# Stick-breaking attention computed for two heads at a time on the tensor array, with paired filter taps and a reordered Hyena stage

## The chip, the cores and the metric

The kernel runs on one core of one Trainium2 chip. The metric is the device time of one execution in microseconds (us), smaller is better; the figure used is the median of several executions.

## The reference, cut to what matters

Two transformer blocks run one after the other on 512 tokens of width 1024, in fp32. The parts that the change touches:

```python
# block 1: 8 heads of 64; attention over strictly earlier tokens
z = q @ k.T * 64 ** -0.5                       # per head, 512 x 512, lower triangle by blocks of 128
log_not = where(s < t, log_sigmoid(-z), 0)
suffix  = reverse_cumsum(log_not) - log_not
a = where(s < t, exp(log_sigmoid(z) + suffix), 0)
o = a @ v
# block 2: differential attention (4 heads, two score maps of 64 each, 512 x 768) beside a Hyena mixer
s = q @ k.T * 64 ** -0.5; a = softmax(s); w = a[0] - lam * a[1]
h = sin(freq * (z @ w1 + b1)); h = sin(freq * (h @ w2 + b2)); h = sin(freq * (h @ w3 + b3)); h = h @ w4
z = gate * (long_conv(z, fft(h)) + skip * z)   # twice, on 3 * 512 projected channels with a short convolution
```

Projections, branch gates, two feed-forward layers and the norms around them fill the rest of the time and are not touched.

## The kernel before

All matrix products are kept near fp32 accuracy: an operand is split into a high and a low half (`..h`, `..l`, wh, wl), and `mm3` issues high times high, high times low and low times high. Weights stream in units of 1,024 columns through four raw buffers and four slots: SyncE issues the load, ScalarE makes wh (L1081), VectorE makes wl (L1651), and for the units listed in `POOL_LOW` GpSimd makes wl instead (L2274). Units of the DFT matrices (kind `pre`) come ready-made by DMA from GpSimd's queue. Every engine has its own program, a fixed list in order; semaphores join them. Nothing is reordered at run time: an engine that waits holds back all that is written behind the wait.

**Filter taps.** `first(k)` and `second(k)` for k = 0 to 19 interleave the input projections with small side work. `filter_layer` makes three sine layers of 64 channels. `taps(i, o)` then issues, for d = 0 and 1, one plain fp32 matmul that contracts over 64 channels, both from partitions 0 to 63. A plain fp32 matmul shows as two records in the trace. VectorE multiplies each result by a decay, GpSimd forms sum and difference (L2311). Steps k = 16 to 19 are `mix`.

**Stick-breaking attention.** A step n is one head h and one block s of 128 keys; its width w is 512 minus 128 s queries, so w = 128, 256, 384, 512 in the order s = 3, 2, 1, 0. The list SB runs head by head, 32 steps. For each step:

- TensorE `scores(n)`: three fp32r matmuls over 64 partitions (0 to 63 for even heads, 64 to 127 for odd ones), into one of four PSUM banks (ZB).
- ScalarE: Abs, Exp, Ln (L1173, L1175, L1177). VectorE: softplus (L1764). GpSimd: the triangular mask (L2344). VectorE: high and low half (L1768, L1770).
- TensorE `later_keys(n)`: products with the constant matrices NEG add the suffix sums to the same bank.
- ScalarE: Exp (L1184). GpSimd: mask. TensorE `values(n)`: one plain fp32 matmul with 64 output partitions.

The order is `scores(n)`, `later_keys(n - 2)`, one `early` part (two k-tiles of a gate projection, six matmuls; 24 parts in all), `values(n - 4)`. The bank of step n is free again when its second Exp (`sb_e2`) is done.

**Differential attention.** `diff_scores(n)` already issues the two maps of a head in turns, map 0 from partitions 0 to 63 and map 1 from 64 to 127. VectorE takes two row maxima (L2062), each followed by a small multiply by -0.125 (L2064), ScalarE the exponentials (L1444), VectorE the weighted difference of the maps (L2076, both operands in SBUF). Two parts of the Hyena projections lie between steps. Units are converted in odd steps, the short convolution (L2083) runs in even ones.

**Hyena stage.** Twelve column groups of the projection (24 matmuls each) are needed. Eight are computed inside the differential attention, groups 8 and 9 at the start of the Hyena stage, group 10 before the last two inverse steps of order 0, group 11 after them. Each order runs `forward` for four frequency blocks, VectorE's products with the spectrum (`spectral`, L2158 to L2162), and `backward`. Between the orders, a chain over ScalarE, VectorE and GpSimd (`acc`, gate, `fold(1)`) makes the input of order 1.

Of the kernel before, what the change touches and what calls it, by code (L numbers as in the profile page):

```python
# [18 lines left out]
BEFORE = 10  # L19
# [8 lines left out]
def plan():  # L28
# [69 lines left out]
    for o in range(2):  # L98
# [48 lines left out]
for _u in range(NU):  # L147
# [9 lines left out]
    AT["dft_f", 0, 0][0][0] + SLOTS - 1 <= u < AT["w_out_2", 0, 0][0][0] + SLOTS - 1  # L157
# [8 lines left out]
class Waits:  # L166
# [5 lines left out]
    def wait_ge(self, name, n):  # L172
        s, before = self.find(name)
        if n > 0 and self.past.get(s.name, 0) < before + n:
# [30 lines left out]
          "high": (("qk_hi", 8), ("mx_hi", 4), ("ot_hi", 8), ("ef_hi", 4), ("g_hi", 12), ("ff_hi", 32), ("qk2_hi", 8),  # L205
                   ("ys_hi", 16), ("ug_hi", 22)),
          "low": (("qk_lo", 8), ("mx_lo", 4), ("ot_lo", 8), ("g_lo", 12), ("qk2_lo", 8)),
          "v_side": (("f_red", 21), ("tap_mul", 16), ("pg_pool", 4), ("gm_nv", 4), ("mx_z", 2)),
          "v_gate": (("eg_raw", 6), ("eg_mul", 4), ("ef_v", 8), ("g_mul", 18)),
          "v_score": (("sb_sp", 32), ("df_mx", 64)),  # L210
# [61 lines left out]
def program(nc, a):  # L272
    ctx = ExitStack()
    with ctx:
# [54 lines left out]
        W4 = at("w4", 168, [64, CHUNK])  # L329
        NEG = at("neg", 174, [P, 2, P], F32R)  # L330
# [39 lines left out]
        EG = [BC[0][:, 0:S], BC[0][:, S:], BC[1][:, S:], BC[1][:, 0:S], T(6), T(7)]  # L370
# [5 lines left out]
        SB = [(h, s) for h in range(8) for s in (3, 2, 1, 0)]  # L376
# [15 lines left out]


# [31 lines left out]
        def tensor_program(engine):  # L425
# [131 lines left out]
            def filter_layer(l):  # L557
# [7 lines left out]
                mm(PS[0:64, b, :], TMP[0:n, 1, 64 * l:64 * l + 64], src, True, True).then_inc(sem("p_filt"), 1)  # L565
# [39 lines left out]
            def scores(n):  # L605
                h, s = SB[n]
                w, t0 = S - P * s, P * s
                pr = slice(64 * (h % 2), 64 * (h % 2) + 64)
                b = bank(("z", n), "sb_e2", n + 1, ZB)
                e.wait_ge("qk_lo", 8)  # L610
                kk = (QKh[pr, 4 + h // 2, t0:t0 + P], QKl[pr, 4 + h // 2, t0:t0 + P])
                mm3(PS[:, b, :w], kk, (QKh[pr, h // 2, t0:], QKl[pr, h // 2, t0:]), True, True).then_inc(sem("p_sc"), 1)
# [14 lines left out]
            def values(n):  # L627
                h, s = SB[n]
                w, t0 = S - P * s, P * s
                pr = slice(64 * (h % 2), 64 * (h % 2) + 64)  # L630
                if s == 3:
                    bank(("o", h), "ot_lo", h + 1, OB)
                e.wait_ge("v_ev", 4)
                e.wait_ge("sb_k2", n + 1)
                mm(PS[pr, BANK["o", h], t0:], V1[:, s, h * 64:h * 64 + 64], T(3 + n % 3, w), s == 3,
                   s == 0).then_inc(sem("p_val"), 1)
# [14 lines left out]
            for k in range(20):  # L651
                if k >= 18:
                    scores(k - 18)
                first(k)
                second(k)


            for n in range(len(SB) + 4):
                if 2 <= n < len(SB):
                    scores(n)  # L660
                if 0 <= n - 2 < len(SB):
                    later_keys(n - 2)
                if n % 3 < 2:
                    early(n - (n + 1) // 3)
                if 0 <= n - 4 < len(SB):
                    values(n - 4)
# [9 lines left out]
            for m in range(EARLY):  # L676
                b = bank(("ef", m), "ef_v", 4 * m + 1)
                for k in range(4):
                    e.wait_ge("ot_lo", 2 * k + 2)
# [283 lines left out]
            for j in range(4):  # L963
                hyena_turn(j)
# [1782 lines left out]
```

## Time and profile before

| | |
|---|---|
| median of 3 executions | 1582.85 us (1582.1 to 1583.59) |
| profiled execution | 1580.21 us, its span 1578.5 us |
| TensorE busy | 1507.5 us, 96% |
| VectorE busy | 877.3 us, 56% |
| ScalarE busy | 622.5 us, 39% |
| GpSimd busy | 291.1 us, 18% |
| granted TensorE clock, mean | 0.991 |
| attention of block 1, 145.6 to 250.5 us | 104.9 us |
| differential attention, 945 to 1052 us | 107 us |
| Hyena stage, 1057.2 to 1153.4 us | 96.2 us |

Busy times are sums over instructions. The span is the profiled stretch on the core; the execution's own time adds 1.7 us around it. TensorE matmuls are pipelined: a record of 0.39 us is followed by the next after about 0.23 us, so what a matmul costs is the distance from its start to the next start, and not its duration.

### The profile page before, as it was taken

What the parts mean: (1) busy time and instruction counts of PE and PEld (TensorE: products, weight loads), DVE (VectorE), ACT (ScalarE), POOL (GpSimd) and SP (SyncE); (2) the same over time, 40 slices, a digit from 0 to 9 for tenths busy, and PEclk for the clock granted to TensorE, in tenths of its full rate; (3) what the DMA queues carried; (4) which work ended last, traced back from release to release, by engine and by line L of the source; (5) the groups of instructions that cost most, each with busy time, mean ns of one, the idle gap of its engine ahead of it and who ended that gap; (6) DMA issues with size and microseconds to landing.
All of it is one profiled execution on the core that took longest, in us unless ns stands there. A gap on an engine that the chain in (4) does not pass through costs nothing.

```text
span 1578.5 us, 17718 instructions
## 1 busy us (share of the span) xinstructions
PE 1507.5 (96%) x6878; PEld 1200.0 (76%) x6878; DVE 877.3 (56%) x1429; ACT 622.5 (39%) x978; POOL 291.1 (18%) x289
## 2 busy tenths in 40 slices
PE   6999999999989999999997998989798999999998
PEld 5767667888868878888886876668576888888886
DVE  5445556555467654565447438856766455334534
ACT  5535664222353322334335325644344333223332
POOL 0253111110122200122004310006441110111101
PEclk9999999999999999999999999999999999999999
DMA  7342002654345544545326221124442322323221
GB/s 232 126 146 81 27 28 93 235 166 148 132 134 173 174 147 140 178 145 178 113 100 208 91 67 40 41 94 139 131 154 69 108 93 95 99 89 106 94 94 54
DMA packets 53262, 187.87 MB, mean 119 GB/s; under 512 B 6104, under 2 KB 6616, under 8 KB 52986
## 3 DMA queue, kind: packets, MB, share of 16 engines
q1 hardware_dynamic: 47386, 165.76, 32.3%
q0 software_dynamic: 4736, 16.78, 3.2%
q10 hardware_dynamic: 1056, 4.19, 0.7%
q8 instruction: 55, 0.90, 0.2%
q14 instruction: 29, 0.24, 0.0%
HBM read 174.12 MB, written 12.58 MB: 118 GB/s over the span
## 4 chain that ended last, share of the span: by engine, by line
PE 80%; DVE 9%; issue 4%; ACT 4%; POOL 3%; DMA 0%; SPq 0%; DVEq 0%; POOLq 0%; ACTq 0%
PE PS L447 79%; POOL TMP L2311 2%; DVE smallring L2062 1%; DVE TMP L2083 1%; PE PS L458 1%; ACT em L1444 1%; DVE wl L1651 1%; DVE TMP L2158 1%; DVE em L2076 1%; POOL y L2321 0%; DMA X<-in_x 0%; ACT wh L1081 0%; DVE accm L1631 0%; ACT wt L1435 0%; POOL wl L2274 0%
## 5 line engine op out<-in xcount | busy, mean ns | idle before, releaser
L1651 DVE TENSOR_TENSOR wl<-raw,wh 128x1024 fp32r<-128x1024 f32 x219 | 283.8, 1299 | 283.1 <-ACT wh L1081 283.0
L447 PE MATMUL PS<-HTh,wh 128*128 128x512 f32 x1056 | 419.7, 397 | 12.4 <-DVE TMP L1977 5.8
L447 PE MATMUL PS<-HTh,wl 128*128 128x512 f32 x1056 | 413.0, 391 | 0.0
L447 PE MATMUL PS<-HTl,wh 128*128 128x512 f32 x1056 | 412.8, 391 | 0.0
L1081 ACT ACTIVATE wh<-raw 128x1024 fp32r<-128x1024 f32 x228 | 239.1, 1053 | 286.2 <-PE PS L447 251.9
L447 PEld LDWEIGHTS PS<-HTh,wh 128*128 128x128 f32 x1056 | 199.5, 189 | 61.3 <-issue 11.0
L447 PEld LDWEIGHTS PS<-HTh,wl 128*128 128x128 f32 x1056 | 199.0, 188 | 42.8
L447 PEld LDWEIGHTS PS<-HTl,wh 128*128 128x128 f32 x1056 | 199.5, 189 | 38.5 <-issue 0.5
L447 PE MATMUL PS<-wh,FFh 128*128 128x512 f32 x432 | 169.1, 392 | 0.0
L447 PE MATMUL PS<-wh,FFl 128*128 128x512 f32 x432 | 168.2, 389 | 0.0
L447 PE MATMUL PS<-wl,FFh 128*128 128x512 f32 x432 | 168.1, 389 | 0.0
L1631 DVE SCALAR_TENSOR_TENSOR accm<-raw,small,accm 128x256 f32<-128x256 f32 x224 | 108.0, 516 | 3.4
L2234 DVE SCALAR_TENSOR_TENSOR TMP<-PS,pp,TMP 128x255 f32<-128x255 f32 (+1 forms) x132 | 52.1, 395 | 80.3 <-ACT TMP L1583 76.4
L447 PEld LDWEIGHTS PS<-wh,FFl 128*128 128x128 f32 x432 | 81.1, 188 | 17.1
L447 PEld LDWEIGHTS PS<-wl,FFh 128*128 128x128 f32 x432 | 81.1, 188 | 16.5
L447 PEld LDWEIGHTS PS<-wh,FFh 128*128 128x128 f32 x432 | 81.1, 188 | 16.5
L2384 POOL TENSOR_TENSOR FFl<-TMP,FFh 128x512 fp32r<-128x512 f32 x32 | 41.6, 1299 | 240.1 <-ACT FFh L1295 240.1
L2466 POOL TENSOR_TENSOR FFl<-TMP,FFh 128x512 fp32r<-128x512 f32 x22 | 28.5, 1294 | 211.8 <-ACT FFh L1590 211.8
L1295 ACT ACTIVATE FFh<-TMP 128x512 fp32r<-128x512 f32 x32 | 20.2, 632 | 66.5 <-DVE TMP L1917 66.5
L1291 ACT ACTIVATE TMP<-PS 128x512 f32<-128x512 f32 x32 | 19.0, 595 | 57.7 <-PE PS L447 57.7
L2083 DVE SCALAR_TENSOR_TENSOR TMP<-PS,pp,TMP 128x255 f32<-128x255 f32 (+1 forms) x72 | 28.4, 395 | 16.0 <-ACT TMP L1452 13.9
L2474 POOL TENSOR_TENSOR X<-X,TMP 128x512 f32<-128x512 f32 x14 | 19.7, 1434 | 90.1 <-DVE TMP L2249 90.1
(320 smaller groups left out, 2163.7 us busy)
## 6 DMA issues: line engine op xcount, KB each, us to landing
raw<-in_ws SPq DMA_DIRECT2D x268, 512.0 KB, 3.8
taps<-TMP SPq DMA_DIRECT2D x16, 256.0 KB, 2.5
tab<-in_spec POOLq DMA_DIRECT2D x8, 512.0 KB, 5.6
raw<-taps SPq DMA_DIRECT2D x8, 512.0 KB, 3.7
kd<-TMP POOLq DMA_DIRECT2D x16, 256.0 KB, 4.3
wh<-in_wd POOLq DMA_DIRECT2D x8, 512.0 KB, 3.9
wl<-in_wd POOLq DMA_DIRECT2D x8, 512.0 KB, 4.6
kf<-kd SPq DMA_DIRECT2D x8, 512.0 KB, 3.9
```

The lines of the kernel that those rows point to most:

```text
L447: return nc.tensor.matmul(out, l, r, start=start, stop=stop, skip_group_check=True)
L1081: act(WH[u % SLOTS][:, :n], RAW[i % RAWS][:, :n], ACT.Copy).then_inc(sem("w_hi"), 1)
L1291: act(T(q % 2), PS[:, BANK["ff", hf, m], :], ACT.Relu).then_inc(sem("ff_relu"), 1)
L1295: act(FFh[:, m, :], T(2 + q % 2), ACT.Copy).then_inc(sem("ff_hi"), 1)
L1631: stt(acc, r[:, k % 4, :], c, acc, ALU.mult, ALU.add).then_inc(sem("mod_acc"), 1)
L1651: tt(WL[k][:, :n], RAW[RAW_AT["unit", u, 0] % RAWS][:, :n], f32(WH[k][:, :n]), ALU.subtract).then_inc(sem("lo_dve"), 1)
L2083: stt(out[:, do], ps[:, di], pp("hy_conv_w_2", 12 * w + j), out[:, do], ALU.mult, ALU.add).then_inc(sem("hc_v"), 1)
L2234: stt(z[:, do], ps[:, di], pp("ffn_conv_w_2", 22 * w + m), z[:, do], ALU.mult, ALU.add).then_inc(sem("uc_v"), 1)
L2311: tt(T(k), T(3), T(5), op).then_inc(sem("tap_ed"), 1)
L2384: tt(FFl[:, q % 16, :], T(2 + q % 2), f32(FFh[:, q % 16, :]), ALU.subtract).then_inc(sem("ff_lo"), 1)
L2466: tt(FFl[:, m - first_m, :], T(m % 4), f32(FFh[:, m - first_m, :]), ALU.subtract).then_inc(sem("ug_lo"), 1)
L2474: tt(x, x, T(4 + q % 4), ALU.add).then_inc(sem("dn_xp"), 1)
```

## The change

- **Two heads at once.** SB now runs over pairs of heads. `scores(p)` issues the three products of the two heads in turns (upper rows, lower rows), `values(p)` two matmuls into output partitions 0 to 63 and 64 to 127 of one bank. The output copy OTh and OTl is made once per pair, on 128 partitions.
- **Order.** `scores(p + 2)` now stands behind `later_keys` and the early parts of pair p, `values(p - 1)` last. There are still four score banks, so `scores(p + 2)` needs both second Exps of pair p.
- **NEG** moves to another address, and its copy from ScalarE's step 14 to step 19, behind the last `mix`.
- **Paired taps.** The filter layers are computed on 128 output partitions (weights and biases repeated), w4 lies as 128 x 1024, and the two matmuls of a tap step contract over the upper and the lower 64 rows.
- **Differential attention.** The scale 0.125 goes into the rotated queries, the maximum is negated by the reduction itself, the small multiply L2064 is gone.
- **Weights' low halves.** POOL_LOW now begins with unit 3 of the Hyena projections instead of unit 3 of the DFT: GpSimd makes wl for groups 3 to 7, and for the later groups.
- **Hyena order.** Group 8 stands before the last two inverse steps of order 0, groups 9 and 10 behind them, group 11 before the last two inverse steps of order 1; their convolutions and transposes move accordingly.

```diff
-BEFORE = 10
+BEFORE = 8
...
-        if o == 0:
-            pack(colmajor("w_in_2", 1536 + 10 * P, 1))
+        pack(colmajor("w_in_2", 1536 + (8 if o == 0 else 11) * P, 1))
         pack(inv[2] + inv[3], "pre")
         if o == 0:
-            pack(colmajor("w_in_2", 1536 + 11 * P, 1))
+            pack(colmajor("w_in_2", 1536 + 9 * P, 2))
...
 POOL_LOW = [u for u in range(NU) if u not in PRE and (
-    AT["dft_f", 0, 0][0][0] + SLOTS - 1 <= u < AT["w_out_2", 0, 0][0][0] + SLOTS - 1
+    AT["w_in_2", 0, 1536][0][0] + SLOTS - 1 <= u < AT["w_out_2", 0, 0][0][0] + SLOTS - 1
...
-        SB = [(h, s) for h in range(8) for s in (3, 2, 1, 0)]
+        SB = [(2 * p + i, s) for p in range(4) for s in (3, 2, 1, 0) for i in range(2)]
...
             def taps(i, o):
+                n = 4 * i + 2 * o
                 for d in range(2):
-                    n = 4 * i + 2 * o + d
-                    b = bank(("tap", n), "tap_mul", n + 1, RING2)
-                    c = o * 1024 + d * 512
-                    e.wait_ge("f_sin", 3)
-                    e.wait_ge("d_w4", 48)
-                    mm(PS[:, b, :], TMP[0:64, 4, i * P:(i + 1) * P], W4[:, c:c + 512], True, True).then_inc(sem("p_tap"), 1)
+                    bank(("tap", n + d), "tap_mul", n + d + 1, RING2)
+                e.wait_ge("f_sin", 3)
+                e.wait_ge("d_w4", 48)
+                for d in range(2):
+                    pr = slice(64 * d, 64 * d + 64)
+                    mm(PS[:, BANK["tap", n + d], :], TMP[pr, 4, i * P:(i + 1) * P], W4[pr, o * S:(o + 1) * S], True,
+                       True).then_inc(sem("p_tap"), 1)
...
+                for i in range(2):
+                    bank(("z", 2 * p + i), "sb_e2", 2 * p + i + 1, ZB)
                 e.wait_ge("qk_lo", 8)
+                for j, (k, q) in enumerate(((QKh, QKh), (QKh, QKl), (QKl, QKh))):
+                    for i in range(2):
+                        pr = slice(64 * i, 64 * i + 64)
+                        m = mm(PS[:, BANK["z", 2 * p + i], :w], k[pr, 4 + c, t0:t0 + P], q[pr, c, t0:], j == 0, j == 2)
...
+                for i in range(2):
+                    c = (h + i) * 64
+                    mm(PS[64 * i:64 * i + 64, BANK["o", h // 2], t0:], V1[:, s, c:c + 64], T(3 + (2 * p + i) % 4, w), s == 3,
+                       s == 0).then_inc(sem("p_val"), 1)
...
+            for p in range(PAIRS + 1):
+                if p < PAIRS:
+                    later_keys(2 * p)
+                    later_keys(2 * p + 1)
+                    for f in EARLY_AT(p):
+                        early(f)
+                if p + 2 < PAIRS:
+                    scores(p + 2)
+                if p:
+                    values(p - 1)
...
-                    nc.vector.reduce_max(r[:, m:m + 1], s, axis=mybir.AxisListType.X).then_inc(sem("df_mx"), 1)
-                    e.wait_ge("df_mx", 4 * n + 2 * m + 1)
-                    ts(r[:, m:m + 1], r[:, m:m + 1], -0.125, None, ALU.mult).then_inc(sem("df_mx"), 1)
+                    nc.vector.reduce_max(r[:, m:m + 1], s, axis=mybir.AxisListType.X, negate=True).then_inc(sem("df_mx"), 1)
...
-                if o == 0:
-                    hyena_group(10)
+                hyena_group(8 + 3 * o)
                 backward(o, 2)
                 backward(o, 3)
+                hyena_turn(8 + 3 * o)
                 if o == 0:
-                    hyena_group(11)
+                    hyena_group(9)
+                    hyena_group(10)
                     sub_scale(2)
```

## Rows read from the trace of the kernel before

**Rows 1.** The page, busy time, share of the span and instructions of each engine.

```profile
PE 1507.5 (96%) x6878; PEld 1200.0 (76%) x6878; DVE 877.3 (56%) x1429; ACT 622.5 (39%) x978; POOL 291.1 (18%) x289
```

**Rows 2.** Windows over four stages: length, busy time of each engine, clock, DMA.

```profile
145.60:250.50 104.90, 103.75 (x462) 66.08 (x458) 58.62 (x114) 65.36 (x140) 19.11 (x64) 1.00 0.10 31
945.00:1052.00 107.00, 94.60 (x517) 69.27 (x517) 84.39 (x176) 59.49 (x103) 1.13 (x2) 1.00 0.18 55
1057.20:1106.90 49.70, 49.70 (x246) 41.22 (x245) 29.49 (x52) 23.08 (x44) 26.18 (x24) 0.97 0.45 147
1106.90:1153.40 46.50, 33.96 (x133) 24.52 (x132) 34.85 (x51) 16.01 (x27) 26.38 (x20) 0.93 0.36 115
```

**Rows 3.** Timeline of TensorE in block 1's attention: start, duration, instruction.

```profile
162.19 0.86 PE L447 MATMUL PS<-TMP,V 128*64 128x384 f32 x2
162.98 0.49 PE L447 MATMUL PS<-QKh 64*128 64x512 f32 x1
...
163.87 0.33 PE L447 MATMUL PS<-sph,neg 128*128 128x128 f32 x1
...
165.92 1.07 PE L447 MATMUL PS<-TMP,V 128*64 128x512 f32 x2
166.92 0.32 PE L447 MATMUL PS<-QKh 64*128 64x128 f32 x1
...
167.40 0.33 PE L447 MATMUL PS<-sph,neg 128*128 128x128 f32 x1
```

**Rows 4.** Timeline of TensorE at small matmuls: taps, two mix steps, differential scores.

```profile
65.16 1.98 PE L447 MATMUL PS<-w,TMP 64*128 64x512 f32 x4
...
131.77 1.07 PE L447 MATMUL PS<-pt,wpool 64*64 64x512 f32 x4
...
140.16 1.09 PE L447 MATMUL PS<-wst,bc 128*64 128x128 f32 x16
...
970.43 0.50 PE L447 MATMUL PS<-KTh,QTh 64*128 64x512 f32 x2
```

**Rows 5.** Groups of ScalarE instructions, 145.6 to 250.5 us.

```profile
L1177 ACT ACTIVATE TMP<-TMP 128x384 f32<-128x384 f32 (+3 forms) x30 | 14.3, 478 | 1.0
L1184 ACT ACTIVATE TMP<-PS 128x128 f32<-128x128 f32 (+3 forms) x32 | 13.7, 427 | 3.3 <-PE PS L447 3.1
L1173 ACT ACTIVATE TMP<-PS 128x384 f32<-128x384 f32 (+3 forms) x30 | 13.2, 442 | 24.0 <-PE PS L447 23.9
```

**Rows 6.** Timeline of TensorE at the start of that attention.

```profile
154.30 0.33 PE L447 MATMUL PS<-sph,neg 128*128 128x128 f32 x1 [1.15 <-DVE spl L1770]
```

**Rows 7.** Timeline of GpSimd, the gate of the second mix.

```profile
147.86 1.28 POOL L2353 TENSOR_TENSOR TMP<-TMP,gu 128x512 f32<-128x512 f32 x1 [1.47 <-DVE TMP L1732]
```

**Rows 8.** Groups of VectorE instructions, 945 to 1052 us.

```profile
L2064 DVE TENSOR_SCALAR smallring<-smallring 128x1 f32<-128x1 f32 x32 | 4.9, 154 | 1.1
```

**Rows 9.** Timeline of ScalarE, VectorE, GpSimd: one unit's conversion, two subtracts, a GpSimd subtract.

```profile
970.17 1.06 ACT L1081 ACTIVATE wh<-raw 128x1024 fp32r<-128x1024 f32 x1
...
972.00 1.02 DVE L2076 SCALAR_TENSOR_TENSOR em<-em,smallring,em 128x768 f32<-128x768 f32 x1
...
1083.41 0.68 DVE L2162 TENSOR_TENSOR TMP<-TMP 128x512 f32<-128x512 f32 x1
...
1095.70 2.83 POOL L2274 TENSOR_TENSOR wl<-raw,wh 128x1024 fp32r<-128x1024 f32 x1
...
1096.20 2.88 DVE L2162 TENSOR_TENSOR TMP<-TMP 128x512 f32<-128x512 f32 x1
```

**Rows 10.** Timeline of ScalarE at the start of the Hyena stage.

```profile
1067.64 2.04 ACT L1475 ACTIVATE U<-PS 128x512 f32<-128x512 f32 x4
1069.70 1.28 ACT L1502 ACT_TABLE_LOAD   x1
```

**Rows 11.** Timeline of TensorE between the orders of the Hyena stage.

```profile
1126.95 2.07 PE L447 MATMUL PS<-ndg,cst 128*128 128x512 f32 x2 [5.01 <-DVE TMP L2083]
...
1150.58 0.50 PE L447 MATMUL PS<-ysh,wh 128*128 128x512 f32 x1 [3.05 <-POOL ysl L2432]
```

More of the change, by code:

```diff
@@ L390, in program, with EARLY_AT @@
                 (0, slice(256, 511), slice(257, 512)), (2, slice(257, 512), slice(256, 511)))
+        PAIRS = len(SB) // 2
+        def EARLY_AT(p):
+            return range((3 * p + 1) // 2, (3 * p + 4) // 2)
         def HSLOT(j):
@@ L651, in tensor_program @@
             for k in range(20):
-                if k >= 18:
-                    scores(k - 18)
+                if k == 18:
+                    scores(0)
                 first(k)
                 second(k)
[L658 to L666, printed above, removed]
+            scores(1)
+            for p in range(PAIRS + 1):
[8 more added lines that the diff above has]
+                    values(p - 1)
             for q in range(4):
@@ L961, in sub_scale @@
                 mm(PS[:, b, :], ONES, NDG[:, :], True, True).then_inc(sem("p_sn"), 1)
-            for j in range(4):
-                hyena_turn(j)
-            hyena_group(8)
-            for j in range(4, 8):
+            for j in range(8):
                 hyena_turn(j)
             sub_sums()
-            hyena_group(9)
-            hyena_turn(8)
             def forward(o, f):
@@ L1198, in scalar_program @@
             for k in range(20):
-                if k >= 18:
-                    scores(k - 18)
+                if k == 18:
+                    for i in range(2):
+                        scores(i)
                 first(k)
                 second(k)
-            for n in range(len(SB) + 4):
-                if 2 <= n < len(SB):
-                    scores(n)
-                if 0 <= n - 2 < len(SB):
-                    later_keys(n - 2)
-                if n % 3 < 2:
-                    early(n - (n + 1) // 3)
-                if 0 <= n - 4 < len(SB):
-                    values(n - 4)
+            for i in range(2, 4):
+                scores(i)
+            for p in range(PAIRS + 1):
+                if p < PAIRS:
+                    later_keys(2 * p)
+                    later_keys(2 * p + 1)
+                    for f in EARLY_AT(p):
+                        early(f)
+                if p + 2 < PAIRS:
+                    scores(2 * p + 4)
+                    scores(2 * p + 5)
+                if p:
+                    values(p - 1)
             weights(unit("w_br_pool", 0, P) + SLOTS - 1)
@@ L1791, in vector_program @@
                 first(k)
-                if k >= 18:
-                    scores(k - 18)
+                if k == 18:
+                    for i in range(2):
+                        scores(i)
                 second(k)
-            for n in range(len(SB) + 4):
-                if 2 <= n < len(SB):
-                    scores(n)
-                if n % 3 < 2:
-                    early(n - (n + 1) // 3)
-                if 0 <= n - 4 < len(SB):
-                    values(n - 4)
+            for i in range(2, 4):
+                scores(i)
+            for p in range(PAIRS + 1):
+                if p < PAIRS:
+                    for f in EARLY_AT(p):
+                        early(f)
+                if p + 2 < PAIRS:
+                    scores(2 * p + 4)
+                    scores(2 * p + 5)
+                if p:
+                    values(p - 1)
             weights(unit("w_br_pool", 0, P) + SLOTS - 1)
@@ L2717 @@
         elif n.startswith("hy_b") or n == "hy_freq_2":
-            ppv[0:64, o] = i[n].reshape(-1)
+            ppv[:, o] = np.tile(i[n].reshape(-1), 2)
         else:
@@ L2731 @@
         "lam": np.concatenate([i[n].reshape(-1) for n in ("lam_q1_2", "lam_q2_2", "lam_k1_2", "lam_k2_2")]),
[L2732 to L2734 removed]
+        "hy_w4_2": i["hy_w4_2"][0].reshape(64, 2, 2, S).transpose(2, 0, 1, 3).reshape(P, D),
+    }
+    for n in ("hy_w1_2", "hy_w2_2", "hy_w3_2"):
+        arrays[n] = np.tile(i[n][0], (1, 2))
     arrays = {k: np.ascontiguousarray(v) for k, v in arrays.items()}
```

181 lines of the change are left out of this document (83 added, 98 removed).

## The prediction

> **What bounds the kernel now.** I read the page first: TensorE is busy for 1507.5 of 1578.5 us [rows 1], so work taken off TensorE comes out of the span wherever TensorE doesn't wait. Then a table of windows shows where it waits. In the attention of block 1 (145.6 to 250.5 us) TensorE is busy 103.75 of 104.9 us while ScalarE works 65.36 and VectorE 58.62 [rows 2]: TensorE is the limit, with about a third of ScalarE's time in reserve. In the differential attention it is busy 94.60 of 107 us, and VectorE 84.39 [rows 2]: there a VectorE and ScalarE chain sets the pace at several steps. In the second half of the Hyena stage it is busy 33.96 of 46.50 us, so 12.5 us are waits; in the first half it never waits (49.70 of 49.70) [rows 2]. The rest of the kernel isn't edited. The timeline gives the price of single matmuls, as start to next start.
>
> **Taps.** Today a tap step is four records of 1.98 us, of which the last 0.07 overlaps what follows: 1.91 us [rows 4]. Is a pair in two halves of the array concurrent? The mix step at 131.77 us does that now: four records of the same width, two matmuls in opposite 64 x 64 quarters, in 1.07 us against 1.98 [rows 4]. I take 0.86 us saved for each of eight steps, 6.8 us (bounds: 0 if the form with all 128 columns didn't overlap, 7.3 at 0.91 each). Both banks are now awaited at once; the old second matmul had waited for the same multiply, and steps lie some 7 us apart, so nothing is late. GpSimd's running sums start when the last tap is out, so they move forward with TensorE. The sine layers with 128 outputs stream as many columns as before, and their DMAs are small: nothing.
>
> **Attention of block 1, TensorE's part.** The value matmul of width 384 costs 162.98 - 162.19 = 0.79 us, of width 512 166.92 - 165.92 = 1.00 [rows 3]; by this step of 0.21 the other widths are 0.58 and 0.37, 2.74 us per head. The score step of width 512 costs 163.87 - 162.98 = 0.89, of width 128 167.40 - 166.92 = 0.48 [rows 3]; the widths between, by a straight line, 0.75 and 0.62, also 2.74 per head. Eight heads: 21.9 us of each. Does pairing halve them? For scores the trace holds the new form itself: the differential scores issue two fp32r matmuls from upper and lower rows, and the pair of width 512 takes 0.50 us [rows 4], as long as the single one (0.49 [rows 3]), and the next pair starts 0.3 us later. So 10.95 us. For values the nearest row is the mix at 140.16: sixteen records of width 128 alternate between left and right columns in 1.09 us [rows 4], where the two records of a lone value matmul of that width need 0.37, so 0.064 us a record against about 0.18. So 10.95 us again, together 21.9. Bounds: 10.95 if only scores overlap; 23.3 if the switch into and out of the small form, about 0.09 us, is also saved on half the steps beyond what the slots contain.
>
> Here the Trainium skill, "TensorE: Matmul & The Clock Gate", section "Measured speedup vs the span model", gives less: three column tiles reached 2.38 times, 0.79 per tile. By that rate a pair is 1.59 times as fast, and values would save 8.1 us where the rows give 10.95; no row of width 512 in this form settles it.
>
> **The same stage, the other engines.** Two things are new. First, ScalarE and TensorE are now coupled once per pair: `scores(p + 2)` needs the second Exps of pair p, which stand on ScalarE behind the three functions of pair p + 1. ScalarE needs 0.442 + 0.478 + 0.478 + 0.427 = 1.83 us per step (Exp and Ln alike) [rows 5], 3.65 per pair; with TensorE's score pair (0.69) and two handoffs, some 0.3, the loop is 4.6 us. TensorE's own pair costs (104.9 - 21.9) / 16 = 5.2 us. On average TensorE stays the limit, but the widest pair takes about 1.35 times ScalarE's mean, 4.9 + 0.9 + 0.3 = 6.1 us, and meets an iteration of TensorE with little work (one early part, short `later_keys`): about 4 to 4.7. The iterations beside it have slack, so I charge 0.65 us per head pair, 2.6 us. Second, NEG. `later_keys(0)` now waits for a copy behind the last mix: VectorE's addition (about 0.6), GpSimd's product 1.28 [rows 7], two ScalarE copies (about 1.0) and handoffs (0.4), 3.3 us after the mix, less 0.6 for the score pair in between, 2.7 us idle where 1.15 is idle now [rows 6]: 1.6 lost. The stage's gain: 21.9 - 2.6 - 1.6 = 17.7 us (bounds 7 and 22).
>
> **Differential attention.** 32 multiplies of 0.154 us vanish, 4.9 us in all [rows 8]; start to start each costs about 0.13, 0.27 per step, and it counts in the 11 or so steps that VectorE paces: 3.0 us. The move of wl is a loss. VectorE's wl (odd steps) lies in time in which VectorE waits for the second exponential anyway, so taking it away gives nothing. On GpSimd it takes 2.4 to 2.83 us, and while it runs a VectorE operation with both operands in SBUF stands still: L2162 took 2.88 us beside GpSimd's 2.83, alone 0.68 [rows 9]. The conversion wh ends at 971.23, GpSimd would run to about 973.7, and VectorE's L2076, both operands in SBUF, is due at 972.00 for 1.02 us [rows 9]; it would end at about 974.6 instead of 973.0. That is 1.6 us in a chain that paces TensorE. Five units move (groups 3 to 7); by where their wh ends, three meet L2076: 4.7 us. Net loss 1.7, of which the steps with a value product absorb part: I take 1.0 lost (bounds: 3 gained if nothing collides, 5 lost if all five do).
>
> The Trainium skill, "SBUF — State Buffer", section "SBUF: two separate sides", states the same as a rule and so speaks against this part: VectorE with two SBUF inputs and GpSimd share an exclusive pair of ports, and the loser blocks for a whole instruction. The trace agrees (2.88 beside 0.68).
>
> **Hyena stage.** Groups 8 and 9 leave the first half, 24 matmuls of 0.227 us each, 10.9 us, where TensorE never waits. Two covers go with them. `forward(0, 0)` needs banks that ScalarE frees after its fold copies: about 0.6 us idle. `sub_scale(0)` follows a chain with four copies of 2.04 us and a table load of 1.28 [rows 10], which group 9 hid: about 2.3 us idle. In the second half groups 9 and 10 fill the time of the fold where group 11 alone stood, and VectorE has one convolution ahead of `spectral(4)` instead of two: the waits of 5.01 and 3.05 [rows 11] go, about 5.5 us of group 9 or 10 and 5.4 of group 11 take their place. The 12.5 us of waits are enough for the 10.9 us, but little is left over, and turn 8 and turn 11 now precede the copies that start the fold: even. Gain 10.9 - 0.6 - 2.3 = 8.0 us (bounds 3 and 11).
>
> **Sum.** 6.8 + 17.7 - 1.0 + 8.0 = 31.5 us. The profiled execution took 1580.2 us, so 1548.7; the median shown lies 2.6 higher, at 1582.85: forecast 1551.3 us. Measured differences under 0.2% (3 us) say nothing here.
>
> **Rivals.**
> - **The coupling to ScalarE paces the attention** (loop per pair near 5.9 us instead of 5.2). The handoffs that I put at 0.3 speak for or against it: ScalarE at 58.4 of then 85 us is no bound by itself. Stage gain 8 instead of 17.7: 1561. Chance 0.15.
> - **Values or taps don't overlap in their new form** (128 rows by 64 columns, width 512): 10.95 or 6.8 less, 1558 to 1562. The mix rows speak against it. Chance 0.07. The page's rate of 1.59 alone would give 1554, inside my forecast.
> - **GpSimd meets nothing in the differential attention, and the Hyena gaps close better**: 4 and 3 us more, 1544. Chance 0.17.
> - **The Hyena order gives back what it takes** (a fold starved by the turns before it, the first half's waits longer): 5 less or nothing at all, 1557 to 1559. Chance 0.05.
> - **Slower: only one pair in flight.** If the four banks let no score pair start before the former pair's second Exps were through, a pair would take its whole latency: scores 0.7, ScalarE's three functions 2.8, VectorE and GpSimd about 2, `later_keys` 1.6, Exp 0.9, handoffs 0.5, 8.5 us; sixteen make 136 us for 104.9, 31 lost against 13.8 gained elsewhere: 1600. It decides from 7.4 us per pair on ((104.9 + 13.8) / 16). Four banks hold two pairs, so it should not come. Chance 0.03.
>
> **How the numbers follow.** The forecast has 0.53; its own range is 1546 to 1556. The range of 0.8 takes in the ScalarE loop and the better Hyena case: 1542 to 1563. Faster by over 0.2%: all but the slow case and a remnant, 0.95; same 0.02; slower 0.03.
>
> **What the profile after would show.** Tap steps of about 1.07 us for four records; score pairs that start about 0.9 us (width 512) before what follows; value records x4 in 1.07 us; the stage of block 1 about 87 us, with short waits on ScalarE's L1184 group at the widest pairs and one of 2.7 us before the first `later_keys`; L2064 gone; L2076 of 2.6 us at some steps beside GpSimd's L2274; TensorE waiting 2 to 3 us early in the Hyena stage and no more 5 us between the orders. I am wrong if value pairs stay at twice 1.00 us, if ScalarE holds every pair, or if the differential attention changes by more than 5 us.

## The result, and the profile after

The changed kernel takes 1557.43 us (median of 4, 1555.99 to 1559.42) against 1582.59 in the same comparison: ratio 0.9841 [0.9826, 0.9855], 25.2 us faster. The forecast was 1551.3 us, with a range of 1542 to 1563. The profiled execution took 1557.35 us, its span 1555.6.

The page of the changed kernel, busy time, share and instructions, beside [rows 1]:

```profile
PE 1482.2 (95%) x6878; PEld 1191.4 (77%) x6878; DVE 864.5 (56%) x1386; ACT 619.0 (40%) x974; POOL 308.7 (20%) x296
```

The windows over the same stages, beside [rows 2]; block 1's attention, the differential attention, and the two parts of the Hyena stage. Columns: length, busy time of TensorE, its weight loads, VectorE, ScalarE, GpSimd, granted clock, DMA share, GB/s.

```profile
137.50:227.10 89.60, 81.49 (x465) 58.73 (x461) 54.04 (x108) 62.70 (x138) 20.24 (x64) 0.98 0.11 36
...
920.50:1040.70 120.20, 106.27 (x528) 74.41 (x529) 78.13 (x137) 57.23 (x101) 14.92 (x9) 0.94 0.15 49
1040.70:1081.80 41.10, 38.05 (x186) 30.80 (x185) 30.30 (x46) 22.54 (x42) 26.46 (x21) 0.96 0.40 129
1081.80:1130.30 48.50, 43.97 (x185) 34.46 (x184) 33.88 (x57) 18.33 (x30) 30.12 (x24) 0.96 0.46 152
```

From the last mix matmul to the end of its attention, block 1 went from 104.9 to 89.6 us, and TensorE now waits there for 8 us. The differential attention, cut at the same matmuls in both, went from 112.2 to 120.2 us: it got **slower by 8 us**, at a granted clock of 0.94 (1 is 2.4 GHz, 0.5 is 1.2 GHz) where it had 1.00. From there to the last normalisation, 107.1 us became 102.6.

The new forms on TensorE in the timeline, beside [rows 3, 4]: values of width 384 and 512, a score pair of width 384, a tap step.

```profile
97.24 1.13 PE L453 MATMUL PS<-w,TMP 64*128 64x512 f32 x4
98.30 0.50 PE L453 MATMUL PS<-HTh,wh 128*128 128x512 f32 x1
...
163.90 0.87 PE L453 MATMUL PS<-TMP,V 128*64 128x384 f32 x4
164.70 0.33 PE L453 MATMUL PS<-sph,neg 128*128 128x128 f32 x1
...
168.08 0.44 PE L453 MATMUL PS<-QKh 64*128 64x384 f32 x2
168.35 0.33 PE L453 MATMUL PS<-QKl,QKh 64*128 64x384 f32 x2
168.52 0.34 PE L453 MATMUL PS<-QKh,QKl 64*128 64x384 f32 x2
168.79 1.08 PE L453 MATMUL PS<-TMP,V 128*64 128x512 f32 x4
169.80 0.33 PE L453 MATMUL PS<-sph,neg 128*128 128x128 f32 x1
```

Start to next start, two heads' values now take 0.80 and 1.01 us where one head's took 0.79 and 1.00; a score pair of width 384 takes 0.71, as one head's did before (148.63 to 149.34 us there), where the prediction had put 0.75 between its rows; a tap step takes 1.06 in place of 1.91. So a pair costs what one costs, to within 0.02 us for values and scores, and a tap step is 0.10 us more than half of the old one. The rate of three column tiles (of 32 columns each) that the prediction cited from the Trainium skill ("TensorE: Matmul & The Clock Gate", "Measured speedup vs the span model"), 1.59 for a pair, does not carry over to two tiles of 64 columns: 2 x 1.00 / 1.01 = 1.98 here.

The start of the attention in TensorE's timeline; in brackets how long it sat idle before, and for whom. One wait was foreseen there, for NEG:

```profile
136.66 1.09 PE L453 MATMUL PS<-wst,bc 128*64 128x128 f32 x16
141.03 0.39 PE L453 MATMUL PS<-QKh 64*128 64x256 f32 x2 [3.27 <-ACT V L1145]
...
142.73 0.30 PE L453 MATMUL PS<-sph,neg 128*128 128x128 f32 x1 [1.08 <-ACT neg L1176]
...
144.37 0.63 PE L453 MATMUL PS<-HTh,wl 128*128 128x512 f32 x1
144.79 0.63 PE L453 MATMUL PS<-HTh,wh 128*128 128x512 f32 x1
...
146.46 0.39 PE L453 MATMUL PS<-HTl,wh 128*128 128x512 f32 x1
146.69 0.39 PE L453 MATMUL PS<-HTh,wl 128*128 128x512 f32 x1
```

`scores(1)` needs banks that hold block 1's V, and ScalarE evicts them only behind its copy of the mix, which waits for GpSimd:

```profile
138.31 0.63 ACT L1174 ACTIVATE OTh<-TMP 128x512 fp32r<-128x512 f32 x1 [5.55 <-POOL TMP L2372]
138.84 2.04 ACT L1145 ACTIVATE V<-PS 128x512 f32<-128x512 f32 x4
```

Behind the two waits six matmuls run at 0.43 us each, the 1.2 GHz level, where they cost 0.23 at 2.4 GHz: another 1.3 us. The whole stretch at that level lasts 3.4 us (142.9 to 146.3), so it costs 1.7.

The differential attention in the timelines of VectorE, GpSimd and TensorE, in this order:

```profile
948.27 0.27 DVE L2093 TENSOR_SCALAR smallring<-smallring,rd,small 128x1 f32<-128x1 f32 x1
948.58 2.93 DVE L2095 SCALAR_TENSOR_TENSOR em<-em,smallring,em 128x768 f32<-128x768 f32 x1
951.43 1.81 DVE L2083 TENSOR_REDUCE smallring<-PS 128x1 f32<-128x768 f32 x2
```
```profile
948.30 2.39 POOL L2289 TENSOR_TENSOR wl<-raw,wh 128x1024 fp32r<-128x1024 f32 x1 [9.51 <-ACT wh L1095]
```
```profile
954.43 0.49 PE L453 MATMUL PS<-KTh,QTh 64*128 64x512 f32 x2 [2.12 <-ACT em L1464]
```

This is the collision foretold from [rows 9]: L2095 (L2076 before), a product of two SBUF operands, takes 2.93 us beside GpSimd's subtraction and 1.02 alone. It happens three times, at 936.7, 948.6 and 979.0 us, the number that was foretold. Each time the reductions behind it, and so ScalarE's exponentials and TensorE's next scores, come late. The subtractions of the other two units that moved, at 926.21 and 968.99 us, meet L2095 too, but it has begun 0.5 us before them. Then it keeps its 1.02 us, and GpSimd's takes 2.79 and 2.77 in place of 2.39. So the one that starts second is held up. VectorE's row and GpSimd's:

```profile
968.50 1.02 DVE L2095 SCALAR_TENSOR_TENSOR em<-em,smallring,em 128x768 f32<-128x768 f32 x1
```
```profile
968.99 2.77 POOL L2289 TENSOR_TENSOR wl<-raw,wh 128x1024 fp32r<-128x1024 f32 x1 [18.29 <-ACT wh L1095]
```

### The profile page after: what moved, and what is told of

The parts are those of the page before. It is cut to its first block, busy times and chain, and to the rows that moved or that the text cites. A ratio compares the mean times of both kernels' runs of the same rounds, so it can differ in the third digit from the quotient of the medians.

```text
span 1555.6 us, 17697 instructions
## 1 busy us (share of the span) xinstructions
PE 1482.2 (95%) x6878; PEld 1191.4 (77%) x6878; DVE 864.5 (56%) x1386; ACT 619.0 (40%) x974; POOL 308.7 (20%) x296
## 4 chain that ended last, share of the span: by engine, by line
PE 84%; DVE 8%; ACT 5%; issue 2%; POOL 1%; DMA 0%; SPq 0%; ACTq 0%; DVEq 0%; POOLq 0%
PE PS L453 83%; ACT em L1464 1%; DVE TMP L2102 1%; DVE em L2095 1%; DVE TMP L2173 1%; PE PS L464 1%; DVE wl L1666 1%; DVE smallring L2083 1%; DVE TMP L1719 0%; ACT wh L1095 0%; DMA X<-in_x 0%; DVE accm L1646 0%; ACT TMP L1189 0%; POOL wl L2289 0%; ACT wt L1455 0%
## 5 line engine op out<-in xcount | busy, mean ns | idle before, releaser
L1666 DVE TENSOR_TENSOR wl<-raw,wh 128x1024 fp32r<-128x1024 f32 x212 | 274.4, 1299 | 281.8 <-ACT wh L1095 281.3
L2249 DVE SCALAR_TENSOR_TENSOR TMP<-PS,pp,TMP 128x255 f32<-128x255 f32 (+1 forms) x132 | 52.1, 394 | 78.4 <-ACT TMP L1598 74.5
L2289 POOL TENSOR_TENSOR wl<-raw,wh 128x1024 fp32r<-128x1024 f32 x16 | 39.5, 2468 | 123.7 <-ACT wh L1095 123.7
```

What stands on the lines that cost most here:

```text
L1666: tt(WL[k][:, :n], RAW[RAW_AT["unit", u, 0] % RAWS][:, :n], f32(WH[k][:, :n]), ALU.subtract).then_inc(sem("lo_dve"), 1)
L2249: stt(z[:, do], ps[:, di], pp("ffn_conv_w_2", 22 * w + m), z[:, do], ALU.mult, ALU.add).then_inc(sem("uc_v"), 1)
L2289: tt(WL[k][:, :n], RAW[RAW_AT["unit", u, 0] % RAWS][:, :n], f32(WH[k][:, :n]), ALU.subtract).then_inc(sem("lo_pool"), 1)
```

## The experiments

Medians are of 4 or 5 executions, of 12 for the negated maximum. The kernel before had medians of 1581.6 to 1582.6 us in the various comparisons. The 95% interval of a ratio is 2 to 3 us of kernel time to either side (1.3 for the negated maximum), so medians of two versions that are less than about 3 us apart don't tell them apart. The traces say more about single stages. But stretches in which TensorE runs at 1.2 GHz come and go from one trace to another, 1.7 us or 3.4 us each.

**Groups 3 to 7 back on VectorE**, the rest as changed:

```diff
-    AT["w_in_2", 0, 1536][0][0] + SLOTS - 1 <= u < ...
+    AT["dft_f", 0, 0][0][0] <= u < ...
```

> The changed kernel, with one part taken back: VectorE again makes the low halves of the weights of Hyena groups 3 to 7 (five units), GpSimd keeps the later ones. Theory (port and clock): in the changed kernel the weighted difference of the maps took 2.9 us instead of 1.02 at three steps beside GpSimd's subtract, and three stretches at half clock (1.2 GHz) stand in the same stage, where the kernel before had none. Both should go: 3 x 1.9 us and about 3 x 1.4 us, 8 to 10 us faster than the changed kernel, so 1547 to 1550 us; from the first differential scores to the first Hyena transpose about 110 us instead of 120.2. Rival 1 (VectorE's own load): with five conversions back on VectorE, which paces this stage, the gain is eaten, within 2 us of 1557.4. Rival 2 (only the port): 5.7 us faster, 1551.7, the half-clock stretches stay.

Measured: 1549.27 us (1548.29 to 1549.46), ratio 0.9791 [0.9776, 0.9805], 8.2 us faster than the changed kernel. Windows of the stage, and TensorE's waits in it, first this kernel's, then the changed kernel's:

```profile
923.10:1031.60 108.50, 99.87 (x529) 71.49 (x530) 77.67 (x142) 57.09 (x101) 2.20 (x4) 1.00 0.16 54
```
```profile
PE PS L453 <- ACT em L1464: 4.0, 8, 0.9
```
```profile
PE PS L453 <- ACT em L1464: 9.2, 7, 2.1
```

The time is inside the range of the theory. The stage is 11.7 us shorter than in the changed kernel. 5.2 us of that are waits for ScalarE's exponentials; the rest is the clock, since TensorE's busy time for the same matmuls falls from 106.27 to 99.87 us, 6.4 us, and 5.2 + 6.4 = 11.6. Not all of the 6.4 belongs to the collisions. The changed kernel's stage has four stretches at 1.2 GHz, of about 3.4 us and so 1.7 us lost each. Windows behind the first, second and third collision, then at the other two places:

```profile
942.50:946.00 3.50, 3.47 (x25) 3.07 (x26) 3.43 (x6) 1.86 (x3) 0.00 (x0) 1.00 0.00 0
955.40:958.70 3.30, 3.30 (x10) 1.52 (x8) 2.27 (x3) 0.00 (x0) 0.00 (x0) 0.50 0.02 5
986.10:989.40 3.30, 3.30 (x6) 1.51 (x5) 1.94 (x3) 0.00 (x0) 0.00 (x0) 0.50 0.02 5
...
921.20:924.70 3.50, 3.50 (x16) 2.74 (x13) 2.34 (x6) 1.88 (x5) 0.00 (x0) 0.51 0.00 0
...
1034.00:1037.00 3.00, 3.00 (x4) 1.22 (x5) 0.24 (x1) 0.00 (x0) 0.00 (x0) 0.50 0.00 0
```

TensorE waits 2.13, 2.12 and 2.13 us behind the three collisions, and only the second and third wait are followed by the low level. All five traces of kernels with this edit and the paired attention agree in this, and none of the seven traces without the edit has a low stretch at these places.

The stretch at 921 us lies ahead of every collision; five of the thirteen traces have it, two of them of kernels without the edit. The one at 1034 us stands in three of the five and its cause is open. So what the traces tie to the three collisions is 5.2 us of waits and 2 x 1.7 us of clock, 8.6 us, close to the 8.2 us by which the kernels differ. (Two of the runs below, scores head by head and both taps from the lower rows, have the stretch at the start and not the one at 1034 us: their stage takes 118.4 us, against 109.5 in the two kernels without collisions that have the same stretch, 8.9 us.) The clock is two fifths of what a collision costs here.

**That edit alone on the kernel before:**

> The kernel before with one edit of the change alone, the lower bound of POOL_LOW: the low halves of the weights of Hyena groups 3 to 9 go to GpSimd while the differential attention runs. In the changed kernel that edit cost 8.2 us (11.7 in the stage), by three weight products on VectorE that took 2.92 us in place of 1.02 and a low clock behind the waits that follow. Theory: the collision of GpSimd's 2.4 us subtraction with VectorE's product of two SBUF operands is the edit's own and needs nothing else of the change: the stage of the differential attention goes from 112.2 to 120 to 124 us, the kernel to 1588 to 1592 us. Rival: it only costs where VectorE and ScalarE have been sped up around it (the two scalings gone), so that the kernel before has slack for it: 1581 to 1585 us.

Measured: 1591.53 us (1591.44 to 1593.65), ratio 1.0062 [1.0049, 1.0076], 9.6 us slower. Window of the stage, and its waits beside 7.8 us in the kernel before:

```profile
947.40:1070.10 122.70, 104.44 (x528) 74.44 (x529) 83.49 (x169) 59.53 (x103) 19.06 (x9) 0.96 0.15 48
```
```profile
PE PS L447 <- ACT em L1444: 13.7, 9, 2.5
```

122.7 us against 112.2, by 5.9 us more of waits and 4.6 us more of busy time at a clock of 0.96. The edit is a loss of its own; nothing else of the change is needed for it. The rival, slack in the kernel before, fell. It is not quite the loss of the changed kernel, though: in the old order seven units, of groups 3 to 9, are converted in this stage, and GpSimd's subtraction comes first and delays L2076 four times (2.52 to 2.54 us, at 963.7, 975.9, 1006.5 and 1037.2 us). Per collision the stage loses 2.6 us here, and 2.9 by the 8.6 us above.

**The negated maximum alone on the kernel before** (scale in the rotation, L2064 gone):

> The kernel before with one part of the change alone: the factor 0.125 is in the rotation and VectorE's maximum is taken negated, so that the 32 small multiplications of L2064 are gone. The prediction took 3.0 us for it. Theory: VectorE stands on the path of the differential attention, 16 head turns by two of them with some 0.1 us each beside the next instruction: the stage goes from 112.2 to 109.2 to 109.7 us (in the changed kernel with the Hyena part as before it was 109.5) and the kernel to 1579 us (1578 to 1580.5). Rival: the wait for VectorE only passes to the next in the chain, the stage stays within 0.5 us, 1581 to 1583.

Measured: 1578.42 us (1576.62 to 1579.97), ratio 0.9981 [0.9972, 0.9989], 3.5 us faster; the stage takes 108.5 us in place of 112.2. Right, and a little more than the 3.0 foretold. At 0.27 us a step, the 3.7 us of the stage are those of about 14 of the 16 steps, where the prediction had counted 11.

**The Hyena part as before**, with POOL_LOW as before, in the changed kernel:

> The changed kernel with the whole Hyena part as before: groups 8 to 11 of the projection in their old places, their packing and POOL_LOW too. Left of the change are the paired taps, the paired attention and the scaling in the rotation. Theory: by the landmarks the new order gained 4.5 us from the turn to the last normalisation, and GpSimd's earlier subtractions lost 8 us and more in the differential attention; without both the kernel takes the time of the one with groups 3 to 7 on VectorE and 4.5 us more: 1553.8 us (1552.5 to 1555), so a little faster than the changed kernel. Rival A: the order gained its full 8 us and the landmarks hide half of it in the neighbouring stages: 1557 to 1558. Rival B: the new order gives nothing once its own low-clock stretches and the wait of 3.35 us are counted: 1549 to 1551.

Measured: 1556.05 us (1554.42 to 1557.31), ratio 0.9837 [0.9823, 0.985]. My theory (1553.8) lies just outside the interval, and rival A (1557 to 1558) is nearer. Against the kernel with groups 3 to 7 on VectorE, which has the new order and no collision, it is 6.8 us slower, so the new order is worth 6.8 by the medians, where the stage showed 4.5; with intervals of 2 to 3 us the medians alone would not settle it, but the traces agree. The stretch from the Hyena transposes to the last normalisation is 4.7 us longer (107.3 against 102.6), and a wait behind the stage 2.0 us. (The differential attention is 1.0 longer too, 109.5 against 108.5, but that is the low stretch at its start that comes and goes.) The wait, here and in the kernel with the new order:

```profile
1187.48 0.79 PE L454 MATMUL PS<-HTh,wh 128*128 128x512 f32 x1 [5.84 <-DVE TMP L2006]
```
```profile
1178.34 0.80 PE L453 MATMUL PS<-HTh,wh 128*128 128x512 f32 x1 [3.87 <-ACT TMP L1381]
```

It is 5.83 or 5.84 us in all four traces with the old order and 3.87 or 3.88 in all nine with the new. Why was not tried.

**Score matmuls head by head:**

```diff
-                for j, (k, q) in enumerate(((QKh, QKh), (QKh, QKl), (QKl, QKh))):
-                    for i in range(2):
+                for i in range(2):
+                    for j, (k, q) in enumerate(((QKh, QKh), (QKh, QKl), (QKl, QKh))):
```

> The changed kernel, but the six score matmuls of a pair are issued head by head (three from the upper rows, then three from the lower), not in turns. Theory (the overlap comes from alternating halves, and is worth half of the score time): only the third of the one and the first of the other can overlap, so a score pair of width 512 takes about 1.5 us instead of 0.9; over 16 pairs 6 to 9 us slower than 1557.4, less what hides in waits of TensorE for ScalarE. Rival (the halves run independently whatever the order, since each half has its own queue of matmuls): no change, within 1.5 us.

Measured: 1557.99 us (1553.13 to 1558.39), ratio 0.984 [0.9823, 0.9857], the same as the changed kernel; my theory fell and the rival held. Issued as head 0's three, then head 1's three, they still start in pairs:

```profile
167.53 0.45 PE L453 MATMUL PS<-QKh 64*128 64x384 f32 x2
167.81 0.34 PE L453 MATMUL PS<-QKl,QKh 64*128 64x384 f32 x2
167.97 0.34 PE L453 MATMUL PS<-QKh,QKl 64*128 64x384 f32 x2
168.25 1.08 PE L453 MATMUL PS<-TMP,V 128*64 128x512 f32 x4
```

**The two value matmuls of a pair apart**, with the next score pair between them:

```diff
+                if p:
+                    values(p - 1, 0)
                 if p + 2 < PAIRS:
                     scores(p + 2)
                 if p:
-                    values(p - 1)
+                    values(p - 1, 1)
```

> The changed kernel, but the two value matmuls of a pair stand apart, one before the next score pair and one behind it, so they can't overlap. Theory: the overlap of left and right columns is worth 10.95 us, half of 21.9 us of value time, and the parting costs one more switch per pair (0.1 us): 10 to 12.5 us slower than 1557.4 us. Rival (the attention is paced by ScalarE's coupling, not by TensorE): the added TensorE work fills waits of about 1 us per head pair, 5 to 8 us slower.

Measured: 1564.89 us (1559.65 to 1569.77), ratio 0.988 [0.9859, 0.99], 7.5 us slower than the changed kernel; from the first later-keys matmul to the end of the attention 92.8 us in place of 84.4.

```profile
170.26 1.07 PE L453 MATMUL PS<-TMP,V 128*64 128x512 f32 x2
171.27 0.44 PE L453 MATMUL PS<-QKh 64*128 64x384 f32 x2
...
171.99 1.07 PE L453 MATMUL PS<-TMP,V 128*64 128x512 f32 x2
172.99 0.33 PE L453 MATMUL PS<-sph,neg 128*128 128x128 f32 x1
```

Each head's values take a full 1.01 and 1.00 us again. The 8.4 us lost are less than the 10.95 of the term, and for two reasons. The edit parts only 13 of the 16 pairs: for the last three no score pair is left to stand between, so their 2.4 us stay saved and 8.6 can be lost. And, as the rival said, the waits for ScalarE before the widest score pairs shrink and take up part (0.44 us at 176.4, where the run with the scores head by head has 0.79; 1.5 us over the stage). Against that, this trace has a stretch at 1.2 GHz at the start of the attention that is longer by 3 us and costs 1.5 more. 8.6 - 1.5 + 1.5 = 8.6, for the 8.4 measured.

**Both taps of a step from the lower 64 rows:**

```diff
-                    pr = slice(64 * d, 64 * d + 64)
-                    mm(PS[:, BANK["tap", n + d], :], TMP[pr, 4, ...], W4[pr, o * S:(o + 1) * S], True,
+                    c = o * D + d * S
+                    mm(PS[:, BANK["tap", n + d], :], TMP[0:64, 4, ...], W4[:, c:c + S], True,
```

> The changed kernel, but both tap matmuls of a step contract over the same lower 64 rows again, with w4 laid out as before; the sine layers stay 128 wide. Theory: each of the eight steps is 0.85 us longer on TensorE, which has no wait there, 6.8 us slower than 1557.4. Rival (the start of the attention hides it, since ScalarE and GpSimd set when the first score pair and NEG are ready): 3 us slower or less, with the wait after the last mix shorter by the rest.

Measured: 1563.56 us (1558.56 to 1565.96), ratio 0.9878 [0.9858, 0.9899], 6.1 us slower than the changed kernel. From the first tap to the last matmul of the last one 66.4 us in place of 59.7, which is the 66.4 of the kernel before. Row for row as it was:

```profile
64.49 1.98 PE L453 MATMUL PS<-w,TMP 64*128 64x512 f32 x4
```

**Another start of the attention.** NEG at a free address, copied at step 14, and another order at the end of ScalarE's program, where `first(19)` evicts V; VectorE makes both mix additions before the first OTl, and its scores 2 and 3 before the second:

```diff
-        NEG = at("neg", 15, [P, 2, P], F32R)
+        NEG = at("neg", 175, [P, 2, P], F32R)
...
-                if k == 18:
-                    for i in range(2):
-                        scores(i)
-                first(k)
-                second(k)
-            for i in range(2, 4):
-                scores(i)
...
+            scores(0)
+            scores(1)
+            first(18)
+            first(19)
+            second(18)
+            scores(2)
+            scores(3)
+            second(19)
```

> The changed kernel with another order of the work at the start of the attention, and nothing else: NEG lies at a free place and is copied at step 14; ScalarE evicts the four V banks before it waits for GpSimd's first product of the mix; the scores of the second head pair are taken off before the last OTh copy; VectorE adds the second mix before it writes the first OTl. After the change TensorE waited 3.27 us for the last V eviction and 1.08 us for NEG, and ran 6 matmuls at the low clock behind them, 1.31 us. Theory: these waits belong to the order and not to the pairs; all three go, 5.7 us, of which the ScalarE chain of the first pairs takes some back: 1552.5 us (1551 to 1554), and from the last mix matmul to the first later-keys matmul about 1 us in place of 5.25. Rival: TensorE only runs into the next wait, for ScalarE's exponentials of the next pair, so that the stretch from the last mix matmul to the end of the attention (89.6 us) stays, 1556 to 1558 us.

Measured: 1552.22 us (1551.05 to 1554.44), ratio 0.9815 [0.9801, 0.9828], 5.2 us faster than the changed kernel. TensorE's start:

```profile
137.30 1.09 PE L453 MATMUL PS<-wst,bc 128*64 128x128 f32 x16
138.32 0.39 PE L453 MATMUL PS<-QKh 64*128 64x256 f32 x2
...
138.87 0.33 PE L453 MATMUL PS<-sph,neg 128*128 128x128 f32 x1
...
139.65 0.39 PE L453 MATMUL PS<-HTl,wh 128*128 128x512 f32 x1
139.88 0.40 PE L453 MATMUL PS<-HTh,wl 128*128 128x512 f32 x1
```

Both waits are gone, and so is the stretch at 1.2 GHz behind them: the six matmuls step by 0.23 us. All six traces of the paired attention with the old start have that stretch, and none of the four with the new. From the last mix matmul to the first later-keys matmul it takes 0.75 us in place of 5.25.

**Both edits, start and VectorE's low halves:**

> The changed kernel with both edits: the start of the attention in the new order and the low halves of groups 3 to 7 back on VectorE. The two places are 700 us apart and share nothing. Theory: they add, 8.2 us and what the new start alone gives (about 5): 1544 us (1542.5 to 1546), 2.4% below the kernel before. Rival: a part of either was the clock of a stretch that moves elsewhere with the other: 1546.5 to 1549.

Measured: 1544.47 us (1543.99 to 1545.51), ratio 0.9765 [0.9752, 0.9778]. 13.0 us under the changed kernel, 8.2 + 5.2 = 13.4 by the single ones: they add. Its slowest execution (1545.51) is faster than every one of the other versions, except for the last one below, which can't be told from it.

**Two further edits of that version.** Values ahead of the next pair's scores:

> The faster version (early start, low halves of groups 3 to 7 on VectorE; 1544.5 us) with TensorE's value matmuls of a pair ahead of the next pair's score matmuls in place of behind them; no other engine's order changes. TensorE waits there for the score banks, which ScalarE's last exponential frees: 0.7 us, 1.4 us and three times 0.95 in the trace, 4.1 in all. Theory: the value matmuls (1 us or so) fill these waits, 1541 us (1540 to 1542.5). Rival: the scores are what ScalarE's chain begins with, so putting them later only makes ScalarE late for the next pair, and the wait comes back before the later-keys matmuls: 1544 to 1548, no faster or slower.

Measured: 1548.31 us (1546.13 to 1549.04), ratio 0.979 [0.9773, 0.9807], 3.8 slower; that is the rival's outcome, if 0.3 us beyond its range. TensorE's waits in the attention, this kernel and then the one with the early start:

```profile
PE PS L453 <- ACT TMP L1201: 5.8, 5, 1.4
```
```profile
PE PS L453 <- ACT TMP L1201: 4.1, 5, 1.2
```

The waits stand where they stood, before the score pairs, and are 1.7 us longer in all. ScalarE now sits idle for 2.72 us at 177.6 us, before the scores come, where it sat for 0.95 in the version with both edits, so it is late for the pair after. The trace also has two stretches at 1.2 GHz in this attention, behind waits of 1.45 us, where the version with both edits has none; they cost 3.4 us.

VectorE's convolution of group 10 one transform step later:

> The faster version (1544.5 us) with VectorE's convolution of Hyena group 10 one transform step later, behind the products of step 5 in place of ahead of them; nothing else. In the changed kernel TensorE waited there 3.18 us for the products (they read the banks of the transform), the longest wait of the second half of the Hyena stage, and ran 6 matmuls at the low clock behind it. Theory: the convolution's 2.5 us is what the products are late by, and since its turn comes two steps later it can wait: 1541 us (1540 to 1542.5). Rival: VectorE is the bound of this stretch (2.5 us of products a step against 2.3 of TensorE's matmuls), so the wait moves to the next step or to the turn of group 10: 1543.5 to 1546.

Measured: 1544.78 us (1541.49 to 1546.76), ratio 0.977 [0.9753, 0.9787]: no difference; again the rival. (The profiled execution is the fastest of the five, 1541.49 us.) The wait of 3.19 us changed its place and its name:

```profile
1095.32 0.66 PE L464 MATMUL PS<-cst,TMP 128*128 128x128 f32 x4 [2.87 <-DVE TMP L2112]
```

## Why the prediction held, and where it did not

The number missed by 6.1 us of 31.5: inside the range, just outside the forecast's own (1546 to 1556). A single pair in flight, the slower outcome, did not come. That values or taps don't overlap would have given 1558 to 1562; it did not happen either, though the number lies beside it. Most of the miss is one term, the low halves on GpSimd. By its steps:

- **Taps, 6.8:** the stretch of the taps is 6.7 us shorter; undone, they cost 6.1. Right.
- **Attention, TensorE's matmuls, 21.9:** right in kind by the start-to-start times above, and for values by the run with them apart. A little small in size: at full clock TensorE's busy time in the stage fell from 103.75 to 79.8 us (81.49 less the 1.7 of the low stretch), 23.9, above the bound of 23.3. No run took the scores' overlap away, since the one that was meant to didn't.
- **Coupling to ScalarE, 2.6:** right in kind and place (before the pair of width 512), small in size: 3.8 us in four waits. The one other order of TensorE's work that was tried made it worse, by 3.8 us.
- **Start of the attention, 1.6 for NEG:** the step that was wrong in its mechanism. NEG's wait is 1.08 us; in front of it stands one of 3.27 for a bank that still held V, which I had not looked for: before, twelve gate matmuls (2.9 us) ran on TensorE while ScalarE evicted V. The two waits make 4.35 us where the kernel before waited 1.15, and the low clock adds 1.7: 4.9 us lost where 1.6 was foretold. The run with another start got 5.2 us back. The whole stage gained 15.3 where 17.7 was foretold (23.9 - 3.8 - 4.9 = 15.2); the larger gain on TensorE hid part of the two losses, and that was luck.
- **Negated maximum, 3.0:** 3.5. Right.
- **Low halves on GpSimd, 4.7 lost in three collisions:** place, partner and number right, and the stretch too (1.9 us each, foretold 1.6). **The term that was mis-sized is what three collisions cost: 8.2 us in the kernel's time in place of 4.7**, of which I had even taken something off. (It is 9.6 for four of them on the kernel before.) The sum had each delay once; it left out that two of the three waits of 2.1 us are followed by stretches in which TensorE runs at 1.2 GHz, 3.4 us in all. With the 3.5 of the maximum, the runs put this part at 4.7 lost where 1.0 was foretold, just inside the bound of 5 that was meant for five collisions; the 8.0 of the profiled stage contain 3.4 us of low clock that the collisions don't explain. That the two engines exclude each other, and that the one that starts first keeps the ports, is what the Trainium skill, "SBUF — State Buffer", section "SBUF: two separate sides", says. The trace agrees both ways round: L2095 takes 2.93 us when it starts 0.3 us after GpSimd's 2.39, and 1.02 when it starts first.
- **Hyena order, 8.0:** 6.8 on the chip, of which the stage itself shows 4.7 and the wait behind it 2.0. The early waits came, 0.91 and 1.42 us where 2.9 were foretold in all, and the wait of 5.01 is gone. The second half was not even: a wait of 3.18 us for VectorE took its place, and VectorE's load seems to set it, since the run that moved one piece of that load only moved the wait (all waits from the Hyena transposes on: 6.8 us before that move, 8.8 after).

The sum by the chip: taps 6.1, maximum 3.5, order 6.8, low halves -8.2 make 8.2; with 25.2 measured, 17.0 are left for the paired attention, whose stage shows 15.3. Most of these differences have intervals of 3 to 4 us, so the 1.7 between the two says nothing.

## What to carry to other kernels

Pairs of matmuls in two halves of the array, by rows or by columns, cost what one costs, if both stand next to each other; for row halves it was enough that only matmuls of the same half stood between them, and for column halves a score pair in between undid it. Look then at what the engines that release the banks do at the start of the loop, since that took back 8.7 of the 23.9 us saved on TensorE in block 1's attention. Before subtractions go to an idle GpSimd, lay its instruction over VectorE's operations with two SBUF operands; one that is on the way to TensorE cost more than its own delay here. Before a stage's difference between two traces is put down to an edit, look where the low-clock stretches stand in both, and in further traces. Judge a reordering by undoing it on the chip: 2.0 of the 6.7 us that the traces give to the new order lay behind the stage.

## What the runs showed of the hardware

- **The two row halves take their matmuls independently.** Six score matmuls issued head by head start in pairs (167.53, 167.81, 167.97 us), with the steps of the alternating order (168.08, 168.35, 168.52 us), and the stage takes as long (84.3 and 84.4 us).
- **Whichever of VectorE and GpSimd starts first is not held up.** Seen for the product of two SBUF operands beside the subtraction: 2.93 us in place of 1.02 when GpSimd began 0.3 us earlier, and 2.77 to 2.79 in place of 2.39 for GpSimd when VectorE began 0.5 us earlier.
- **Short waits and the clock.** Waits of 3.27 and 1.08 us, and of 2.12 and 2.13, were followed by stretches at 1.2 GHz; the stages without them had a clock of 1.00. It is no simple rule: behind the wait of 2.13 us at 942.5 us the level stayed high, in all five traces that have it; the wait of 1.97 us for V ahead of the differential attention is in all thirteen traces and was followed by a low stretch in five. Behind the wait of 2.87 us in the last run the matmuls stepped by 0.23 us, the high level, while behind 3.19 us at nearly the same place in the version it was made from they went to 0.42 after four more. Which waits bring it is left open.
